# Softmax probabilities of the sliding-window layers: normalised by ScalarE instead of GpSimd

## What is computed

```python
for i in range(DEPTH):
    kind, j = i % N_MIXERS, i // N_MIXERS      # 0 swa, 1 gla, 2 fox, 0 swa
    ...
scores = jnp.einsum('bnqkgd,bnskd->bnkgqs', qb, kb).astype(jnp.float32) * (hd ** -0.5)
...
scores = jnp.where(mask[None, :, None, None], scores, -jnp.inf)
...
probs = jax.nn.softmax(jnp.concatenate([scores, sink_col], axis=-1), axis=-1)[..., :-1]
out = jnp.einsum('bnkgqs,bnskd->bnqkgd', probs.astype(vv.dtype), vv)
```

## Time and profile before

| | us |
|---|---|
| median of 3 executions | 1621.64 (1621.17 to 1627.95) |
| the profiled execution | 1618.61 |
| its span, first to last instruction | 1616.8 |
| TensorE busy | 1554.9 (96%) |
| VectorE busy | 1193.2 (74%) |
| ScalarE busy | 790.4 (49%) |
| GpSimd busy | 94.8 (6%) |

### The profile page before, as it was taken

One profiled execution on the slowest core, in us unless ns is written; L12 is line 12 of the kernel. 1 busy time (PEld: TensorE's weight loads), 2 busy tenths in 40 slices (PEclk: granted clock), 3 DMA queues, 4 the chain that ended last, 5 costly groups with the idle time before them and its releaser, 6 DMA issues.

```text
span 1616.8 us, 30790 instructions
## 1 busy us (share of the span) xinstructions
PE 1554.9 (96%) x12496; PEld 1480.0 (92%) x12496; DVE 1193.2 (74%) x1721; ACT 790.4 (49%) x1040; POOL 94.8 (6%) x105
## 2 busy tenths in 40 slices
PE   2989999999999999999999999999999999999998
PEld 1868999999989999999899999789999898899998
DVE  6898877778378777765587776968777677676665
ACT  2555433356365333455543335565333467655543
POOL 0150000001000000011000000210000013200000
PEclk9989999999999999999999999999999999999999
DMA  9855978755256888573478885446878555345550
GB/s 390 347 193 203 382 295 318 281 203 196 92 209 263 344 300 315 209 284 123 165 296 331 308 313 207 144 157 268 349 300 315 197 182 171 118 160 182 179 182 26
DMA packets 54219, 383.74 MB, mean 237 GB/s; under 512 B 6256, under 2 KB 6512, under 8 KB 8448
## 3 DMA queue, kind: packets, MB, share of 16 engines
q1 hardware_dynamic: 50400, 363.75, 59.4%
q0 software_dynamic: 3744, 18.94, 3.3%
HBM read 378.47 MB, written 4.19 MB: 237 GB/s over the span
## 4 chain that ended last, share of the span: by engine, by line
PE 84%; DVE 9%; DMA 3%; ACT 2%; issue 1%; POOL 1%; SPq 0%; DVEq 0%; ACTq 0%
PE PS L1905 70%; PE PS L1926 4%; DVE wlo L1356 3%; DMA CST<-cst_in 1%; PE PS L2049 1%; PE PS L1975 1%; PE PS L2099 1%; DVE adar L1374 1%; ACT whi L948 1%; DMA adar<-ada 1%; PE PS L2076 1%; DVE SCR L1528 1%; DMA raw<-ada 1%; PE PS L1949 1%; PE PS L1939 1%
## 5 line engine op out<-in xcount | busy, mean ns | idle before, releaser
L1905 PE MATMUL PS<-hhi,whi 128*128 128x256 f32 x2496 | 714.5, 286 | 5.0 <-DVE wlo L1356 2.6
L1356 DVE TENSOR_TENSOR wlo<-raw,whi 128x2048 fp32r<-128x2048 f32 x234 | 536.9, 2296 | 239.7 <-ACT whi L948 239.3
L1905 PE MATMUL PS<-hlo,whi 128*128 128x256 f32 x2496 | 708.2, 284 | 0.0
L1905 PE MATMUL PS<-hhi,wlo 128*128 128x256 f32 x2496 | 708.1, 284 | 0.0
L948 ACT ACTIVATE whi<-raw 128x2048 fp32r<-128x2048 f32 x234 | 447.0, 1911 | 478.4 <-PE PS L1905 465.9
L1905 PEld LDWEIGHTS PS<-hhi,whi 128*128 128x128 f32 x2496 | 481.1, 193 | 11.9 <-issue 7.3
L1905 PEld LDWEIGHTS PS<-hlo,whi 128*128 128x128 f32 x2496 | 481.0, 193 | 1.3 <-issue 1.2
L1905 PEld LDWEIGHTS PS<-hhi,wlo 128*128 128x128 f32 x2496 | 480.9, 193 | 0.0
L1374 DVE CUSTOM_DVE_ANT_0 adar<-adar,CB 128x1024 f32<-128x1024 f32 x232 | 276.9, 1233 | 12.3 <-DMA adar<-ada 12.3
L1905 PE MATMUL PS<-ahi,whi 128*128 128x256 f32 x968 | 274.5, 284 | 1.1 <-DVE alo L1855 1.1
L1905 PE MATMUL PS<-alo,whi 128*128 128x256 f32 x968 | 273.9, 283 | 0.0
(11 more groups left out here) (225 smaller groups left out, 1326.8 us busy)
## 6 DMA issues: line engine op xcount, KB each, us to landing
raw<-weights SPq DMA_DIRECT2D x234, 1024.0 KB, 6.3
adar<-ada SPq DMA_DIRECT2D x104, 1024.0 KB, 5.6
adar<-ada POOLq DMA_DIRECT2D x12, 1024.0 KB, 5.4
raw<-ada SPq DMA_DIRECT2D x4, 1024.0 KB, 14.9
bias_rows<-acc POOLq DMA_DIRECT2D x12, 256.0 KB, 3.5
adar<-bias_rows POOLq DMA_DIRECT2D x8, 256.0 KB, 3.3
CST<-cst_in SPq DMA_DIRECT2D x1, 1128.0 KB, 22.7
CB<-c_in SPq DMA_DIRECT2D x2, 512.0 KB, 4.0
```

What stands on the lines that cost most here:

```text
L1356: v.tensor_tensor(wlo[:, u % CV, :], raw[:, u % RAW, :], whi[:, u % CV, :].bitcast(F32), ALU.subtract).then_inc(lo_done, 1)
L1905: m = pe.matmul(o, w(a), h(b), start=first and k_ == 0, stop=last and k_ == 2, skip_group_check=True)
```

## The change

ScalarE gets a function `normalise(p)` and calls it eight times in a swa layer, at places chosen by hand. It waits for `att_den` and makes four copies within the tile, each 128x128 or 128x256, with one column of reciprocals as the per-partition scale; the last signals `p_norm`. GpSimd's `normalise` is left for layer three (and, in another form, for layer five). Nothing else is moved: TensorE's, VectorE's and SyncE's lists are as they were.

```diff
@@ GpSimd @@
                 if kind in ("swa", "fox"):
                     for p in range(PAIRS):
-                        normalise(p)
+                        if kind == "fox":
+                            normalise(p)
                         if l == 0 and p == 1:
                             first_ada(6, 1)
@@ ScalarE @@
+                def normalise(p):
+
+                    act.wait_ge(att_den, plain0[l] + p + 1)
+                    t, rd = prob_tile(kind, p), stats(kind, p)[3]
+                    for k in range(4):
+                        a, b = segments(kind)[k // 2]
+                        x = t[:, k % 2, a:b]
+                        e = act.activation(x, x, ACT.Copy, scale=rd[:, k:k + 1])
+                    e.then_inc(p_norm, 1)
...
                     exps(0)
                     hi(u0 + 6)
+                    normalise(0)
                     exps(1)
                     hi(u0 + 7)
+                    normalise(1)
                     probs_copy(0)
                     rope_read(4)
                     exps(2)
                     probs_copy(1)
                     rope_read(5)
+                    normalise(2)
                     mixed_hi(0)
                     exps(3)
                     probs_copy(2)
+                    normalise(3)
                     mixed_hi(1)
                     exps(4)
                     mixed_hi(2)
                     probs_copy(3)
+                    normalise(4)
                     hi(u0 + 8)
                     exps(5)
                     mixed_hi(3)
                     probs_copy(4)
+                    normalise(5)
                     exps(6)
                     mixed_hi(4)
                     probs_copy(5)
+                    normalise(6)
                     exps(7)
                     mixed_hi(5)
                     probs_copy(6)
+                    normalise(7)
                     mixed_hi(6)
                     probs_copy(7)
                     mixed_hi(7)
```

## The result

| | before | after |
|---|---|---|
| median | 1621.64 (1621.17 to 1627.95) | 1629.36 (1629.26 to 1634.08) |
| the profiled execution | 1618.61 | 1634.08 |
| its span | 1616.8 | 1632.3 |

Both medians are of five executions; the profiled one of before is a separate, earlier one and shorter than all five. The ratio after to before is 1.005, 95% interval 1.0028 to 1.0072. That is 8.1 us slower with an interval of 4.5 to 11.7, and 7.7 us between the medians, where 6.3 were predicted. So the loss is clear of no change, although it is small.

A forecast was written before the change was run, and what follows sets the result against it. TensorE, busy 96% of the span, was taken as the bound. Layer four +4.5 and layer one -0.8 gave +3.7 at full clock; clock falls +2.6 made +6.3, so 1621.64 + 6.3 = 1627.9 us, range 1621.0 to 1631.5.

The forecast's parts named there:

- What goes: Both layers: GpSimd's three waits (6.7 us), a 0.39 us rotation wait and two clock falls (3.2 us) vanish, 10.3 at most.
- part one: The prediction's account of what GpSimd's multiplications cost on the path: 10.3 us at most, 3.2 of it two clock falls.
- A set of copies: Four ScalarE copies per pair take 1.38 us, between 1.04 and 1.72; the end moves 1.3 us per 0.1.
- `transposes(2)`: Both layers: TensorE waits 2.2 us there, because the copies of pair 2 stand behind `rope_read(5)`.
- Pairs 3 to 5, layer four: `scores(6)` waits 1.1 us, the old 0.39 goes, and `values(4)` comes 3.2 us late.
- The last pairs: Layer four: ScalarE's 4.2 us per pair sets the pace; `values(4)` to `values(7)` takes 12.1 us instead of 10.8.
- Layer four in sum: Layer four's mixer ends 4.5 us late at full clock, plus one clock fall costing up to 1.6.
- Layer one at full clock: Layer one's last `values` at 124.4 instead of 125.18 us, -0.8, as VectorE, no longer stretched, makes up time.
- The clock in layer one: One clock fall counted in layer one, worth 1.0 us because VectorE hides a part.
- the first (the copies are hidden): ScalarE's copies are hidden or cheap, with a 1.04 us set and one clock fall: 1622.0 us; chance 0.11.
- The second: The freed engine decides: every named GpSimd wait goes and nothing replaces it, 1611.3 us; chance 0.03.
- The third: Each longer gap brings a clock fall; four counting in full give +10.1, 1631.7 us; chance 0.24.

The follow-up runs named there:

- e2: The change in layer four only, GpSimd normalising layer one as in the kernel before; 1625.49 us, ratio 1.0028.
- e9: The changed kernel with a constant scale of 0.5 in the copies instead of the reciprocals, output not normalised; 1622.72 us, ratio 1.0017.
- e3: The changed kernel with the copies of pair 2 put ahead of the last rotation read in both layers; 1621.25 us, ratio 1.0006.
- e6: The changed kernel with eight useless matmuls ahead of TensorE's wait at `transposes(2)` in both layers; 1627.52 us, ratio 1.0041.
- e1: The change in layer one only, GpSimd normalising layer four as in the kernel before; 1625.06 us, ratio 1.0011.
- e12: The changed kernel measured again, unaltered, on another chip; 1631.74 us against 1618.82 before, ratio 1.0066.
- e10: The changed kernel with pair 2's copies earlier in layer one, and GpSimd normalising layer four except its last pair; 1619.25 us, ratio 0.9986.
- e11: As e10, with eight useless matmuls in layer one ahead of TensorE's wait before `aux_product(5)`; 1616.05 us, ratio 0.9980.
- e5: The kernel before, GpSimd still normalising, plus equal-sized unused ScalarE copies at the change's places without waiting for reciprocals; 1630.66 us, ratio 1.0055.
- e4: The changed kernel with normalising left out in layers one and four, transposes waiting for reciprocals alone; 1612.22 us, ratio 0.9948.

## Why the prediction was right, and where not

It was right in the sign, in the mechanism of layer four, and in size for the comparison that it was made for: 1627.9 against 1629.36. The second measurement fits less well: 1631.74, just above the range's end of 1631.5, and by its ratio 10.7 us (6.6 to 14.7) slower than before on that chip. By its steps:

- **What goes.** The three waits for GpSimd and the 0.39 us for the rotation are gone, as said. The `lo` that stood beside the last multiplication is short again (2.28 us). The 3.2 us that part one put on two falls in layer one weren't on the path there: in e2, whose layer one is that of before, no fall follows the gap of 3.25 us, the next long wait for GpSimd is 3.46 us instead of 1.83, and the mixer is no shorter.
- **A set of copies.** Predicted 0.497 and 0.391 each and 1.48 with its end; measured 0.503, 0.398, and 1.48 to 1.52. e9 shows the price of the pointer, and that the layer's loss hangs on it: 4.74 - 2.13 = 2.6 us at full clock for 0.38 a set, 0.7 per 0.1 in layer four. In layer one it is 0.15 + 1.50 = 1.65 us, 0.4 per 0.1. Together that is 1.1 per 0.1, where I put 1.3.
- **`transposes(2)`.** Predicted a wait of 2.2 us in both layers, measured 2.12 in both. e3 shows its cause, the place behind `rope_read(5)`.
- **Pairs 3 to 5, layer four.** `scores(6)` waits 0.78, not 1.1. `values(4)` predicted 3.2 us late; in e6, without the fall, it starts 48.07 us after the first rotation product, against 44.55 before: 3.5.
- **The last pairs.** Predicted 4.2, 4.2 and 3.6 from `values` to `values` with waits of 0.6; measured 4.20, 4.19 and 3.62 with waits of 0.51.
- **Layer four in sum.** Predicted 4.5 at full clock and one fall of 1.6, so 6.1; measured 4.74 and 1.62, so 6.36.
- **Layer one at full clock is a term that was mis-sized.** Predicted -0.8; e1 has +0.15 and e12 -0.14, both without a fall in the mixer. Most of it is there at the start of `transposes(2)`: I had 92.4 us, after has 92.67, e12 92.73 and e1 92.94. From there on the carrying forward holds in e1: 14.5 us predicted to `transposes(4)`, 14.59 measured, then 10.4 and 10.39 to `transposes(6)`. What is missing before it is mainly the end of `unit(5)`, which comes 0.6 us later than before in after and e12 and 0.8 in e1, where I had 0.4. The rest is an overlap: before, `transposes(2)` started 0.17 us ahead of the end of the product before it, and behind a gap it can't.
- **The clock in layer one.** Predicted one fall worth 1.0. In after there are 10.2 us of low clock in it (0.52 over 93.3 to 100.1 us, 0.54 over 110.4 to 113.8), 4.8 us of matmul time, and the layer is 1.34 - 0.15 = 1.2 us longer than in e1; in e12 there are none. So a lost microsecond costs about 0.25 there, and the sum came near 1.0 only because there was more low clock than I counted: that is luck. Even this price isn't firm, for e3 and e10 have the same layer one, with 6.8 us of low clock and with none, and differ by 0.2 us. That VectorE hides the rest is argued from the rows: TensorE's next long wait, 2.17 us at `aux_product(5)`, is for it.

In sum 6.2 to 7.7 for the mixers, 6.3 predicted. The 7.7 us between the medians equal the latter, but I don't take that as proof: "between" differs by 5.6 us between the two profiles of the change, and the prediction had nothing for it.

**What lies outside the mixers.** The record has the mean granted clock of each execution, so executions can be compared at the same clock. At 0.991, nineteen executions of before on all chips take 1617.1 to 1619.5 us, mean 1618.6, and the one of the change 1626.27. At 0.989, fifteen of before take 1621.2 to 1623.8, mean 1622.4, and the two of the change 1629.36 and 1628.04; at 0.990 eleven of before take 1618.4 to 1623.3, mean 1619.9, and the two of the change 1629.26 and 1629.27. So at equal clock the change costs 5.6 to 9.4 us, about what the mixers show or somewhat more, and the rest of e12's difference goes with a lower clock.

e1 doesn't fit this: its three executions at 0.991 take 1621.95 to 1622.88, 3.9 us above the mean of before, with mixers only 0.2 us longer (at 0.988 it is 1.3 us). Its profile shows how. Before has its low clock inside layer one (0.93 over 75 to 100 us, 0.86 over 100 to 125). e1 has 1.00 in both, but 0.93 over 125 to 150 and 0.86 over 400 to 425, where before has 1.00 and where TensorE is busy for 22.7 and 25.0 of 25 us, so little or nothing is hidden. Of the fourteen profiles, the nine with a clock below 1.00 over 125 to 150 us all have one over 400 to 425 too, and "between" is +1.5 to +7.2 us; in the other five it is within 0.1. **Open** stays what decides between the two groups: e2, with the layer one of before, is among the nine, and e9 and e11, with ScalarE's copies in layer one, are among the five. So no run shows that the change itself brings the low clock behind layer one.

Of the rivals, the first (the copies are hidden) fails by the 0.51 us rows and by e5; in the form "not at the wrong place" it is half right, for e3 comes out at the time of before. The second would have needed the copies to cost nothing; e4, which leaves them out, is 8.4 us faster. The third needed three falls that count in full; in the mixers there was one in layer four, and the low clock in layer one cost 1.2 us in all. Its rule that each longer gap is followed by a fall is wrong: e12 and e2 have gaps of 2.1 to 3.3 us without one. That e12's median is its 1631.7 is no proof for it, since e12's mixers, in the profile, cost 6.2 us.

## What to carry to other kernels

Before work is moved to an engine that is idle on average, look at its idle time in the stretch where the next engine waits, here 9.83 of 10 us busy against 50% over the span, and at what would stand ahead of the moved work in its order: one step earlier was worth 3.8 us a layer. Look also for the one instance that pays (here the last pair, behind which the engine has nothing more to do: -1.55 us in its mixer). And take the difference of two profiles stage by stage, since the clock can make some us of difference in stages that nobody has touched; but check the whole against executions at the same mean clock, since a stage by stage reading leaves out what moves to another stage.

## What the runs showed of the hardware

- **A gap doesn't decide a clock fall by its length.** The gaps of 2.12 and 2.17 us in layer one were followed by a granted clock of 0.58 in one execution and of 1.00 in another of the same kernel. In before, gaps of 2.69 and 3.25 us had 0.59 and 0.57 behind them; in e2, whose layer one is the same, they had 1.00. Two gaps of e2, and the windows behind them:

```profile
94.33 1.10 PE L2050 MATMUL PS<-SCR,CST 128*128 128x512 f32 x2 [2.69 <-DVE hlo L1589]
...
108.25 0.87 PE L2097 MATMUL PS<-CST,SCR 128*128 128x128 f32 x6 [3.25 <-POOL SCR L891]
```

```profile
94.40:98.40 4.00, 4.00 (x30) 2.70 (x30) 4.00 (x7) 2.06 (x8) 3.85 (x3) 1.00 0.55 229
...
108.30:112.30 4.00, 3.91 (x34) 3.05 (x34) 3.81 (x11) 2.70 (x11) 2.84 (x3) 1.00 0.91 301
```

I had set a gap of 1.83 us with a fall behind it beside one of 1.62 without; the runs show only that gaps of 1.8 to 3.3 us can have one. What differs between the executions isn't in the rows.
- **Falls also come with TensorE busy all the time**: 0.73 over 400 to 425 us with 25.00 us busy, 1.00 there in before. The stretch between the two mixers, which no kernel here changes, is up to 7.2 us longer than in before by falls of this kind and by those behind layer one.
- **GpSimd and VectorE.** With GpSimd out of the swa layers, the rotation multiply of VectorE is back from a mean of 809 ns to 687, and the modulation's dot products from 1233 to 1220 ns:

```profile
L1479 DVE TENSOR_TENSOR SCR<-SCR,CST 128x512 f32<-128x512 f32 x10 | 8.1, 809 | 0.8 <-PE PS L2029 0.6
```

in before, and in after

```profile
L1498 DVE TENSOR_TENSOR SCR<-SCR,CST 128x512 f32<-128x512 f32 x10 | 6.9, 687 | 1.6 <-PE PS L2048 1.3
```

The Trainium skill, page "SBUF — State Buffer", section "Who interferes with whom", says that a VectorE instruction with two SBUF inputs contends with a GpSimd instruction that reads SBUF; the rows agree, for the multiply (0.12 us) more than for the dot products (0.01 us on average over all 232).
